# Moving the sample key scores into the mix projection of a two-layer hybrid decoder step

## What is computed

```python
x = x + 0.5 * swiglu(rmsnorm(x, g_ffn1), f1_in, f1_out)
z = rmsnorm(x, g_mix) @ w_in                       # 1024 -> 2944 columns, "the mix projection"
u, qa, ka, va, qr, kr, vr, gr = jnp.split(z, offs, axis=-1)
y_pool = pool_mixer(u, ...)                        # causal means, windows 2,4,8,16
y_att  = moba(qa, [cache_k; ka], [cache_v; va])    # samples: 1024 cached keys of 6 heads x 64
y_ret  = silu(gr) * rms(retention(qr, kr, vr, s0))
x = x + concat(y_pool, y_att, y_ret) @ w_out
x = x + 0.5 * swiglu(rmsnorm(x, g_ffn2), f2_in, f2_out)
```

## Time and profile before

| | us |
|---|---|
| median of 3 runs (1479.1 to 1491.0) | 1486.24 |
| the profiled execution | 1489.81 |
| its span in the trace | 1487.4 |
| TensorE busy | 1386.3 (93%) |
| VectorE busy | 811.9 (55%) |
| mean granted TensorE clock | 0.947 |

### The profile page before, as it was taken

The page is one execution under the profiler, slowest core; times in us unless marked ns, Lnnn a source line. Parts: engine busy times, 40 slices in busy tenths (PEclk is TensorE's granted clock), DMA queues, the critical chain, the costliest instruction groups (busy, mean ns, idle before and its releaser), DMA issues.

```text
span 1487.4 us, 28349 instructions
## 1 busy us (share of the span) xinstructions
PE 1386.3 (93%) x11165; PEld 1321.5 (89%) x11165; DVE 811.9 (55%) x848; ACT 649.9 (44%) x715; POOL 215.8 (15%) x341
## 2 busy tenths in 40 slices
PE   6999999999856999999999999999995689999998
PEld 5999999998445899999999999999973479999998
DVE  5555544574564465554555554555737536555545
ACT  4555533342312465553355554343423125555433
POOL 3000001530434100000100000036024221000001
PEclk9999999998678999999999999999976799999998
DMA  6444444752577244444444444467346725444443
GB/s 205 144 161 147 134 156 155 213 172 63 177 238 254 95 141 146 161 141 144 144 150 161 142 141 155 143 167 239 101 160 203 260 90 167 143 141 157 143 152 120
DMA packets 210893, 235.25 MB, mean 158 GB/s; under 512 B 14974, under 2 KB 203144, under 8 KB 210804
## 3 DMA queue, kind: packets, MB, share of 16 engines
q1 hardware_dynamic: 200828, 204.90, 42.8%
q0 software_dynamic: 9856, 29.14, 6.1%
q10 hardware_dynamic: 120, 0.03, 0.0%
HBM read 228.83 MB, written 5.32 MB: 157 GB/s over the span
## 4 chain that ended last, share of the span: by engine, by line
PE 85%; DVE 6%; issue 5%; DVEq 1%; ACT 1%; DMA 0%; POOLq 0%; POOL 0%; SPq 0%; ACTq 0%
PE ps L1160 24%; PE ps L1162 24%; PE ps L1161 24%; PE ps L1405 4%; DVE kbuf L941 2%; PE ps L1468 1%; PE ps L1304 1%; DVEq L1091 1%; PE ps L1524 1%; PE ps L1347 1%; PE ps L1266 1%; PE ps L1525 1%; PE ps L1526 1%; PE ps L1315 1%; DVE h_lo L803 0%
## 5 line engine op out<-in xcount | busy, mean ns | idle before, releaser
L546 ACT ACTIVATE w_hi<-w_raw 128x2048 fp32r<-128x2048 f32 x170 | 325.5, 1915 | 536.8 <-PE ps L1162 503.7
L796 DVE TENSOR_TENSOR w_lo<-w_raw,w_hi 128x2048 fp32r<-128x2048 f32 x170 | 392.3, 2308 | 198.1 <-ACT w_hi L546 195.6
L1160 PE MATMUL ps<-h_hi,w_hi 128*128 128x320 f32 x1136 | 358.5, 316 | 10.3 <-DVE w_lo L796 3.5
L1161 PE MATMUL ps<-h_lo,w_hi 128*128 128x320 f32 x1136 | 354.5, 312 | 0.0
L1162 PE MATMUL ps<-h_hi,w_lo 128*128 128x320 f32 x1136 | 354.4, 312 | 0.0
L1160 PEld LDWEIGHTS ps<-h_hi,w_hi 128*128 128x128 f32 x1136 | 216.6, 191 | 14.1 <-DVE h_lo L803 7.0
L1160 PE MATMUL ps<-g_hi,w_hi 128*128 128x320 f32 x704 | 217.5, 309 | 1.2 <-DVE g_lo L803 1.2
L1160 PE MATMUL ps<-act_hi,w_hi 128*128 128x320 f32 x704 | 217.5, 309 | 0.0
L1161 PE MATMUL ps<-act_lo,w_hi 128*128 128x320 f32 x704 | 217.5, 309 | 0.0
L1162 PE MATMUL ps<-act_hi,w_lo 128*128 128x320 f32 x704 | 217.5, 309 | 0.0
L1161 PEld LDWEIGHTS ps<-h_lo,w_hi 128*128 128x128 f32 x1136 | 216.7, 191 | 0.3
(11 more groups left out here) (224 smaller groups left out, 1476.1 us busy)
## 6 DMA issues: line engine op xcount, KB each, us to landing
w_raw<-in_ffn_w_in SPq DMA_DIRECT2D x90, 1024.0 KB, 5.1
w_raw<-in_ffn_w_out SPq DMA_DIRECT2D x32, 896.0 KB, 4.6
kbuf<-in_cache_k SPq DMA_DIRECT2D x128, 192.0 KB, 4.3
vbuf<-in_cache_v POOLq DMA_DIRECT2D x128, 192.0 KB, 4.2
w_raw<-in_w_in SPq DMA_DIRECT2D x22, 1024.0 KB, 5.5
w_raw<-in_ffn_w_out SPq DMA_DIRECT2D x16, 1024.0 KB, 5.0
w_raw<-in_w_out SPq DMA_DIRECT2D x8, 1024.0 KB, 9.2
s<-in_state_ret POOLq DMA_DIRECT2D x12, 128.0 KB, 7.2
```

Of the source, the lines that this page charges most:

```text
L546: act.activation(w_hi[:, slot, :], w_raw[:, slot, :], ACT.Copy).then_inc(hi_done, 1)
L796: dve.tensor_tensor(w_lo[:, slot, :], w_raw[:, slot, :], w_hi[:, slot, :].bitcast(F32), ALU.subtract).then_inc(split_done, 1)
L1160: pe.matmul(out, w_hi[:, slot, w], hi[:, k, :], start=(k == 0), stop=False)
L1161: pe.matmul(out, w_hi[:, slot, w], lo[:, k, :], start=False, stop=False)
```

## The change

Keys. Pair 0 is loaded around the projection's first weights, turned during chunks 2 to 5 and scored after `mix(5)`. Pair 1 is loaded and turned behind it and scored after `mix(9)`. Pair 2 is turned and scored at the projection's end, pair 3 in the tail, after `mean_squares`. The scores write banks 2 to 5, and the probabilities have three homes (`sp_a`, `sp_b`, `sp_c`; pair 3 uses the first again).

Mix. Every chunk now writes banks 0 and 1: tile 0 to bank 0, tile 1 to bank 1. VectorE evicts tile by tile, `evac_first(c)` (waits for `tile_done`, raises `mix_half`) and `evac_last(c)`. Tile 0 of chunk c waits for `evac_first(c-1)`, tile 1 for `evac_last(c-1)`.

Values. The eight samples' values have five homes in the order `"CWABDCAB"`: C and D in the arena, A and B the key buffers after the last scores, W a half of a weight slot and of `w_hi`. The loads wait accordingly. In the tail the order of retention and samples is new, one `w_out` weight chunk is loaded and split later, and `past_states` moves from behind `mix(10)` to behind `scores(2)`, ahead of `mix(9)`.

The core of the diff:

```diff
-                def evac(c):
-                    n, b = (2, 2 * (c % 2)) if c < 11 else (1, 2)
+                def evac_first(c):
+                    dve.wait_ge(tile_done, L * 11 + (c + 1))
+                    dve.tensor_tensor(z[:, 2 * c, :], ps[:, 0, 0:TOK], rstd[:], ALU.mult).then_inc(mix_half, 1)
+
+                def evac_last(c):
                     dve.wait_ge(chunk_used, L * C_ALL + (C_MIX + c + 3))
+                    b = 1 if c < 11 else 0
+                    dve.tensor_tensor(z[:, 2 * c + b, :], ps[:, b, 0:TOK], rstd[:], ALU.mult).then_inc(evac_done, 1)
...
                 def mix(c):
-                    square_group(L, half0 + (C_MIX + c) // 2, G_MIX + c, c % 2, h_hi, h_lo, None if c else gx(norm + 1),
-                                 cols=2 if c < 11 else 1)
+                    chunk_split(half0 + (C_MIX + c) // 2, c % 2)
+                    for a in range(2 if c < 11 else 1):
+                        if c == 0:
+                            banks_free(L, G_MIX)
+                        elif a == 0:
+                            pe.wait_ge(mix_half, L * 11 + c)
+                        else:
+                            pe.wait_ge(evac_done, L * G_ALL + (GROUPS0 + G_MIX + c))
...
                 mix(5)
                 pe.wait_ge(ka_out, 3 * L + 1)
                 tokens(ZKA, 1, 7).then_inc(ka_tr, 1)
+                pe.wait_ge(kown_ok, L + 1)
+                pe.wait_ge(s_max, H * L + 2)
+                sample_scores(0)
                 mix(6)
...
                 mix(9)
                 wait_apart(pe, oa_out, 3 * L + 1)
                 tokens(ZKA, 2, 7).then_inc(ka_tr, 1)
                 transpose_p(3)
+                pe.wait_ge(s_max, H * L + 6)
+                pe.wait_ge(past_ok, L + 1)
+                sample_scores(1)
                 mix(10)
...
+                for half in range(2):
+                    turn_k(3, 0, half)
+                or_norm(0)
+                for half in range(2):
+                    turn_k(3, 1, half)
+                soft_in(3)
+                soft_sum(2)
+                soft_bias(3)
+                or_norm(1)
+                or_norm(2)
+                y_rest(0)
...
+                for f in range(3):
+                    or_high(f)
+                out_evac(0, 0)
+                out_evac(0, 1)
+                probs_evac(1)
+                y_high(0)
```

More of the change, by code:

```diff
@@ L763, in _ @@
+                probs_evac(0)
+                for f in range(3):
+                    or_high(f)
[3 more added lines that the diff above has]
+                y_high(0)
+                exps(3)
+                out_evac(1, 0)
+                out_evac(1, 1)
+                probs_evac(2)
+                y_high(1)
+                out_evac(2, 0)
+                out_evac(2, 1)
+                probs_evac(3)
                 y_high(2)
-                probs_evac(3)
+                mix_hi(13)
@@ L1013, in _ @@
                 normalise(1)
-                evac(6)
-                mix_lo(8)
+                soft_in(0)
+                evac_first(6)
+                soft_bias(0)
+                evac_last(6)
                 smax(2)
@@ L1033, in _ @@
                 ins.then_inc(q_dec_ok, 1)
-                evac(8)
-                mix_lo(10)
+                evac_last(7)
+                normalise(2)
+                normalise(3)
+                mix_lo(9)
+                soft_sum(0)
+                turn_k(1, 0, 0)
+                evac_first(8)
+                turn_k(1, 0, 1)
+                evac_last(8)
                 smax(4)
@@ new lines, in smp_out @@
+                def smp_out(p, bb):
+                    u = 2 * p + bb
+                    if bb == 0:
+                        pe.wait_ge(pt2_evac, L * 8 + p * 2 + 2)
+                        if p:
+                            pe.wait_ge(ys_low, 4 * L + p)
+                    pe.wait_ge(v_landed[V_HOME[u]], v_count(L, u))
+                    for j in range(PAGES + 1):
+                        for f in range(3):
+                            rows = P if j < PAGES else SMP
+                            c = 96 * j + 32 * f
+                            cols = slice(P * f, P * f + P)
+                            v = v_page(u, j, cols) if j < PAGES else v_own[:, cols]
+                            ins = pe.matmul(ps[32 * f:32 * f + 32, 6 + bb, 0:P], pt_s[p % 2][0:rows, c:c + 32], v,
+                                            start=(j == 0), stop=(j == PAGES))
+                    ins.then_inc(pv_done, 1)
@@ L1350, in _, with mean_squares @@
+                def mean_squares():
+                    pe.wait_ge(o_sqd, 3 * L + 3)
+                    for f in range(3):
+                        pe.matmul(ps[:, 2 + f, 0:TOK], head_mean[:], o_sq[:, f, :], start=True, stop=True).then_inc(mean_done, 1)
                 mix(0)
@@ L1409, in own_scores @@
-                def own_scores():
-                    for bb in range(2):
-                        for f in range(3):
-                            ins = pe.matmul(ps[32 * f:32 * f + 32, 7, 256:256 + SMP], q_bd[:, f, bb, :], k_own[:, f, :],
-                                            start=(bb == 0), stop=(bb == 1))
-                    ins.then_inc(own_done, 1)
-                wait_apart(pe, past_ok, L + 1)
+                mixed(12)
                 ret_scores(0)
-                mixed(11)
@@ L1501, in _ @@
+                for t in range(2):
+                    pe.matmul(ps[:, 6 + t, 0:TOK], wbd[:, t, :], tmp[:, 1820 + TOK * t:1820 + TOK * t + TOK],
+                              start=True, stop=True).then_inc(pool_mm, 1)
+                wait_apart(pe, vr_out, 3 * L + 3)
                 ret_scores(2)
-                pe.wait_ge(pool_low, 2 * L + 2)
+                ret_scores(3)
+                wait_apart(pe, pool_low, 2 * L + 1)
                 ret_out(0)
+                wait_apart(pe, pool_low, 2 * L + 2)
```

555 lines of the change are left out of this document (294 added, 261 removed).

## The result

The changed kernel takes 1507.15 us (median of 4 runs, 1506.17 to 1509.59), the kernel before on the same chip 1485.87 (median of 4, 1479.1 to 1491.0). The ratio is 1.0149 with a 95% interval of 1.0106 to 1.0191: slower by 21 us, where 1485 was forecast and 1507 was the upper end of the range. Measured again later beside the kernel before, it was 1.0159 (1.0133 to 1.0185).

What follows compares the result with a forecast made beforehand. TensorE, at 93% of the span, was taken as the bound, so only its holes could shrink. Per layer 33.7 us added less 34.2 saved gave -0.5, -1 for both; forecast 1485 us, range 1464 to 1507.

Steps and rivals of the forecast that it cites:

- At nothing I cost the rest of the projection: Projection: key transposes, first softmax, key loads, SP's new waits and GpSimd's pair 0 preparation were all taken to cost nothing.
- `rstd` ahead of chunk 1: Projection, chunk 1: its tile 0 needs evac_first(0), which needs rstd, leaving TensorE 3.9 us with nothing.
- Head 3's maximum with the split behind it: Projection, ahead of chunk 8: the weight split and evac_first(7) queue behind this maximum on VectorE, a 4.65 us wait.
- Head 5's chain to `past_ok`: Projection, ahead of pair 1's scores: maximum, split, two key transposes, two evictions and a copy on VectorE, 9.3 us.
- Low clock behind the first two: Projection: a low-clock stretch costs 1.8 us, charged behind each of the first two waits, 3.6 us per layer.
- Rival (b): Projection: clock stays at 1.2 GHz for all of chunks 1, 8 and 10; +16.5 us per layer, 1518 us; chance 0.05.
- Pair 0's scores: Projection: pair 0's key scores move in and run at the high clock, adding 4.9 us per layer.
- pair 1's 6.6: Projection: pair 1's key scores move in behind a long wait, first sample at the low clock, adding 6.6 us.
- The tail until the mean squares: Tail's first part: the work of before with pair 2's scores for pair 0's, less one weight split, 36.7 us.
- Rival (a): Tail's start: pair 2's key transposes on VectorE, 7.1 us, delay the retention; about 9.5 us more per layer, 1504; chance 0.18.
- From the mean squares to the late part of `w_out`: Rest of the tail, from 36.7 us to its end at 97.5 us.
- The wait for pair 0's outputs: Tail, after pair 0's value products: TensorE waits ten microseconds because of ScalarE's and VectorE's order.

Runs made afterwards that it cites:

- a3_heads: The changed kernel with the maxima of heads 3 and 5 moved on VectorE behind work that is ready; 1477.6 us, ratio 0.9960 to the kernel before.
- b1_banks: The kernel with three moves (w_out load, spread values, maxima; 1445.5 us), with chunk 1 written to two banks of its own; 1434.7 us, ratio 0.9658.
- c2_between: The changed kernel with the first w_out chunk's load between the key loads of pair 2's two samples; 1493.5 us, ratio 1.0069 to the kernel before.
- a1_load: The changed kernel with the first w_out chunk's load ahead of pair 2's key loads and key store on SP; 1482.3 us, ratio 1.0004.
- b2_tail: The kernel with three moves (1445.5 us), with evictions of pair 0's and 1's outputs ahead of work awaiting the gates' reciprocals; 1445.4 us, ratio 0.9735.

## Why the prediction was wrong

The step that failed is the one that said "At nothing I cost the rest of the projection", in its sentences on SP's queue and on GpSimd. It named "SP's new waits for pair 0's scores" and walked only the weights of the mix behind them. It did not walk SP's list past `mix_load(11)`, where the wait for pair 1's scores stands ahead of the first `w_out` chunk, and it had just put 9.3 us in front of those scores. GpSimd's list was read for pair 0 alone. The closing sentence, that a late weight load would make it wrong to the slow side, is what happened.

Point by point, forecast and measured in layer 1:

- `rstd` ahead of chunk 1: 3.9, measured 3.46. Head 3's maximum with the split behind it: 4.65, measured 4.30. Head 5's chain to `past_ok`: 9.3, measured 9.15. The walk of both engines' orders was right, and a3_heads and b1_banks show the causes.
- Low clock behind the first two: 1.8 each, measured 1.4 and 1.5 by some 12 spaced matmuls behind each. Rival (b), a whole chunk at the low level, did not come. For the Trainium skill, "TensorE: Matmul & The Clock Gate", section "HAM oscillation", an idle gap puts the clock back and the next work pays again; that agrees with each of the three waits paying by itself (the third in pair 1's scores, 6.82 us where pair 0's took 4.29), and in c2_between a wait of 2.94 us left the same low clock as one of 7.78.
- Pair 0's scores 4.9, measured 4.6; pair 1's 6.6, measured 382.41 - 375.31 = 7.1. The projection as a whole: 102.3 + 33.0 = 135.3, measured 134.9.
- The tail until the mean squares: 36.7, measured 439.90 - 394.52 = 45.4. Of these 8.7 the weights' wait is 7.78 and GpSimd's 3.33, less 2.4 that the rest ran faster. Rival (a), VectorE's turns of pair 2, appeared as 0.9 us here.
- From the mean squares to the late part of `w_out`: 97.5 - 36.7 = 60.8, measured 501.85 - 439.90 = 62.0. The wait for pair 0's outputs was forecast as 10 and is 6.60 + 1.21 = 7.8; pair 3's second half (at 453.63) ran in 4.10, the low clock, where 2.5 was forecast. One sum is off by a little: 0.3 + 3.7 + 3.5 ahead of pair 3's scores is 7.5, where the forecast went on with 7.1.

So the two parts of the tail are 8.7 + 1.2 over; less the 0.7 that the forecast had put at the projection's end and the 0.4 by which the projection was shorter, 8.8 are left, but for rounding the gap between the forecast -0.5 and the measured +8.2 of layer 1. The two waits that had no price, 7.78 + 3.33, are more than all of it. The move of one line (a1_load) brings the kernel to 1.0004 of the one before, close to the -1 us that the sum had said. In part that is luck, since GpSimd's wait is still there in that kernel (1.74 us in layer 1, 5.32 in layer 2). The 11.5 us a layer that this move gave are more than 7.78 (6.64 in layer 2), because the wait also lowered the clock for what follows. The forecast had taken this part from the tail of before, where the low clock stood elsewhere. The first two lines are of the kernel before, the others of the changed one, with the granted clock third from the end:

```profile
361.20:368.00 6.80, 6.17 (x124) 4.57 (x121) 3.21 (x7) 2.36 (x5) 0.00 (x0) 1.00 0.55 171
380.00:400.20 20.20, 16.73 (x102) 9.62 (x103) 11.46 (x27) 4.61 (x6) 6.94 (x9) 0.61 0.44 147
```

```profile
402.30:421.00 18.70, 16.88 (x236) 11.94 (x236) 12.96 (x16) 8.13 (x20) 4.22 (x6) 0.56 0.10 21
421.00:440.00 19.00, 14.14 (x127) 8.40 (x125) 9.24 (x25) 3.87 (x7) 9.80 (x20) 0.89 0.82 283
```

Before, the tail began at the high level and its retention ran low; now it begins low, behind the wait, and the retention runs mostly high. The two stretches of low clock about cancel, which fits the 2.4 us by which the rest ran faster, and a gap of 8.7 where the move gave 11.5; no run tests this by itself.

The chances were off as well: 0.21 for slower by over 1%, of which nothing was for a late load. The change in itself was not a bad one. With its lists put in order it is 2.6% faster than the kernel before, and 4.1% with the further moves; no run made such moves in the kernel before, so part of this may be open to it as well. The forecast had priced the waits of heads 3 and 5 as costs of the change. As it was written they were, but only by VectorE's order, which could be had otherwise.

## What to carry to other kernels

When a wait is added to a queue that issues loads in order, walk that queue to its end, and ask of every load behind the wait when its data is needed; a price of nothing is only good for the loads that were walked. An instruction that waits long on an in-order engine is a place to look at for ready work queued behind it: one maximum idled 16.93 us ahead of four steps that could have run meanwhile, and it and its like at head 3 were worth 29 us when moved. And a wait that has been moved away is only worth its length if what comes next is ready: in b2_tail 7.3 us of it bought nothing that could be measured, because the values behind it were still being issued and moved.

## What the runs showed of the hardware

In layer 1 a wait of 2.94 us left TensorE at the low clock just as one of 7.78 did: the same transpositions took 0.82 behind both and 0.49 without. GpSimd alone issued four pages of 192 KB every 2.9 us and moved 249 GB/s with them; with SP issuing values beside it, it was 336 in the same stretch, and 369 in both kernels from 430 to 440, after SP had issued two chunks of 1 MB as well. A page then took a median of 6.1 to 7.4 us to land and not 3.2. So a second queue added throughput where one queue's issuing was the limit, and only time to landing beyond that.
